# Seven block products in four more of group 0's pairs, in a one-core decoder step on Trainium2

## The chip, the cores and the metric

The kernel runs on one core of one Trainium2 chip. The metric is device time in microseconds (us). Three runs of the kernel before gave 2213.06, 2214.12 and 2216.58 us; the median is 2214.12.

## What is computed

One inference step of a two-layer decoder trunk on 576 tokens (8 samples of 8 tokens, then one prompt of 512), 1024 features, in float32. Each layer is a half-weighted SwiGLU feed-forward block (FFN), a mixer, and a second such block; layer 0's mixer is an mLSTM, layer 1's a gated linear attention (GLA). The FFN's hidden width is 2816.

```python
def rmsnorm(x, w):
    y = x * rsqrt(mean(x * x, axis=-1) + EPS)
    return y * w
def swiglu(x, w_gate, w_up, w_down):
    return (silu(x @ w_gate) * (x @ w_up)) @ w_down
for l in range(2):
    x = x + 0.5 * swiglu(rmsnorm(x, norm_w[l, 0]), ...)
    x = x + mixer[l](rmsnorm(x, norm_w[l, 1]))
    x = x + 0.5 * swiglu(rmsnorm(x, norm_w[l, 2]), ...)
out = rmsnorm(x, final_norm_w)
```

## The kernel before

**Number format.** Each float32 operand is split into a high part (fp32r, a ScalarE copy) and a low part (VectorE: value minus high part). A product of two operands is three matmuls: high x high, high x low, low x high. Weights arrive by DMA as blocks of 128 output features (512 KB, 128x1024) in `raw`, four slots; `split` on ScalarE (L1182) and VectorE (L1715) makes `w_hi` and `w_lo`.

**Layout.** Features lie on partitions. The 576 tokens are two halves of 288 columns (`FIRST`, `SECOND`), one PSUM bank each. There are 8 PSUM banks, so a pair of blocks (2 blocks x 2 halves) takes 4, and pairs alternate between banks 0 to 3 and 4 to 7.

**Phases.** An FFN is cut into three groups of 8, 8 and 6 hidden tiles of 128. Each group is a phase G (one pair per hidden tile: a gate block and an up block, evacuated to `h_hi`, `h_lo`) and a phase D (four pairs of w_down blocks, added to x). The FFNs are numbered 0 to 3; 0 and 1 stand around the mLSTM mixer, 2 and 3 around the GLA mixer. `PHASES` is the list of all phases in order; every engine walks it in its own instruction stream, and semaphores with counted values order them. Nothing but these streams and waits sets the order.

**A plain pair** (`feature_pair`, L476): per block 8 feature tiles x 3 matmuls x 2 token halves, 96 matmuls of 128x288 in all. All of phase D and all 8 pairs of group 0's G are plain. They read `xn`, the input times the norm's weights but not yet times 1/rms (`rstd`), because rstd is known only at the end of the first pair (`token_sums`, `norm_rstd`); the factor is applied on evacuation (`evac_g`, L1889 and L1891).

**A seven-product pair** (`seven_pair`, L533), groups 1 and 2 of G. The gate and up matrices, cut in even and odd feature tiles, and the activations, cut in even and odd tiles and in two token halves, are 2x2 block matrices. They are multiplied with seven block products instead of eight (a Winograd form), 7 x 4 x 3 = 84 matmuls of 128x288. That needs sums of weights (`sum_1` to `sum_4`, L1738 to L1758, VectorE, 128x512), their high and low parts (`unit_high` L1197, `unit_low` L1730), sums of activations (`t_sums`, made in phase D of group 0 with rstd already in them, in `th_hi`, `th_lo`), copies of partial results out of PSUM (`product_copy`, L1216) and four additions that join them (`part`, L1772). The last of these and the Silu (L1248, L1250) are followed by `rows_product` (L1780), the high part (L1254) and `rows_low` (L1788).

**The start.** x comes in four pieces of two tiles; ScalarE makes the high part (L1267) and the squares (L1274) of each, and behind the first piece the high parts of the first weight pair. ScalarE's first instruction waits for the norm weights and x.

## Time and profile before

| | |
|---|---|
| profiled execution, its own time | 2216.74 us |
| span | 2215.0 us, mean granted TensorE clock 0.994 |
| TensorE (PE) busy | 2176.4 us, 98%, 16504 matmuls |
| VectorE (DVE) busy | 1433.1 us, 65% |
| ScalarE (ACT) busy | 885.8 us, 40% |
| GpSimd (POOL) busy | 45.7 us, 2% |
| chain that ended last | PE 93%, DVE 4%, ACT 2%, issue 1% |
| costliest lines of the chain | L476 55%, L533 27%, L750 4% |

Times are microseconds from the span's start. An instruction's row has its start, its length, the engine, the line, and output and input with their shapes; "x2" joins two neighbours of one kind; in brackets stand the idle time of the engine before it and what ended that. Instructions of one engine overlap a little, so the spacing of starts is shorter than the lengths. A row of a stage view has the stretch, its length, then for PE, PEld (weight load), DVE, ACT and POOL the busy time and the number of instructions, then the granted TensorE clock (1.00 is 2.4 GHz), the DMA share and GB/s.

### The profile page before, as it was taken

The numbers are of one execution on the slowest core, as the hardware profiler recorded it, in microseconds if no ns is written. First come the engines' busy times: TensorE is split into PE (matmuls) and PEld (weight loads), VectorE is DVE, ScalarE is ACT, GpSimd is POOL, SyncE is SP. The second block draws the span as 40 slices with busy tenths as digits, with TensorE's granted clock in tenths as the row PEclk, the third lists the DMA queues.
The fourth block names the chain that finished last, engine by engine and source line by source line (L and its number), as shares of the span: only waits on it lengthen the run. The fifth ranks groups of instructions, "written<-read, shape, count | busy, mean of one in ns | idle before, by whom it ended". The sixth has DMA issues, their size and how long they took to land.

```text
span 2215.0 us, 40643 instructions
## 1 busy us (share of the span) xinstructions
PE 2176.4 (98%) x16504; PEld 2154.1 (97%) x16504; DVE 1433.1 (65%) x2131; ACT 885.8 (40%) x1366; POOL 45.7 (2%) x50
## 2 busy tenths in 40 slices
PE   7999999999999999999999999999999999999997
PEld 7999999999999999999999999999999899999997
DVE  5488657685555468848655884864766454788485
ACT  4235435354533334525423452544322432345252
POOL 0000000001100000000000000000011100000000
PEclk9999999999999999999999999999999999999999
DMA  5222322223332222222322222232122222223222
GB/s 185 77 81 89 114 67 86 96 88 130 108 114 77 95 77 81 90 87 88 109 80 76 86 95 95 81 100 88 47 96 87 95 77 95 76 86 104 76 86 72
DMA packets 72566, 201.42 MB, mean 91 GB/s; under 512 B 7268, under 2 KB 26980, under 8 KB 72448
## 3 DMA queue, kind: packets, MB, share of 16 engines
q1 hardware_dynamic: 72448, 199.80, 27.6%
q8 instruction: 80, 1.31, 0.2%
q14 instruction: 38, 0.31, 0.1%
HBM read 187.82 MB, written 11.95 MB: 90 GB/s over the span
## 4 chain that ended last, share of the span: by engine, by line
PE 93%; DVE 4%; ACT 2%; issue 1%; DMA 0%; POOL 0%; DVEq 0%; SPq 0%; ACTq 0%; POOLq 0%
PE ps L476 55%; PE ps L533 27%; PE ps L750 4%; PE ps L605 1%; DVE w_lo L1715 1%; PE ps L781 1%; PE ps L770 1%; PE ps L784 0%; PE ps L800 0%; ACT w_hi L1182 0%; PE ps L614 0%; PE ps L793 0%; PE ps L628 0%; PE ps L794 0%; DVE x L2514 0%
## 5 line engine op out<-in xcount | busy, mean ns | idle before, releaser
L476 PE MATMUL ps<-h_lo,w_hi 128*128 128x288 f32 x1616 | 350.9, 294 | 4.1 <-DVE h_hi L2179 4.1
L476 PE MATMUL ps<-h_hi,w_hi 128*128 128x288 f32 x1616 | 350.7, 294 | 2.5 <-DVE w_lo L1715 1.6
L476 PE MATMUL ps<-xn_hi,w_hi 128*128 128x288 f32 x1536 | 337.3, 298 | 12.4 <-DVE w_lo L1715 11.5
L476 PE MATMUL ps<-xn_hi,w_lo 128*128 128x288 f32 x1536 | 332.1, 294 | 0.0
L476 PE MATMUL ps<-xn_lo,w_hi 128*128 128x288 f32 x1536 | 331.8, 294 | 0.0
L1715 DVE TENSOR_TENSOR w_lo<-raw,w_hi 128x1024 fp32r<-128x1024 f32 x220 | 259.4, 1221 | 56.7 <-ACT w_hi L1182 54.5
L476 PE MATMUL ps<-h_hi,w_lo 128*128 128x288 f32 x1360 | 294.0, 293 | 0.0
L476 PEld LDWEIGHTS ps<-xn_hi,w_hi 128*128 128x128 f32 x1536 | 248.1, 189 | 20.5 <-issue 18.0
L476 PEld LDWEIGHTS ps<-h_lo,w_hi 128*128 128x128 f32 x1616 | 261.6, 189 | 4.8 <-DVE h_hi L2179 4.5
L476 PEld LDWEIGHTS ps<-h_hi,w_hi 128*128 128x128 f32 x1616 | 261.5, 189 | 3.5 <-DVE w_lo L1715 1.8
L533 PE MATMUL ps<-th_lo,w_hi 128*128 128x288 f32 x896 | 264.2, 295 | 0.0
L533 PE MATMUL ps<-th_hi,w_lo 128*128 128x288 f32 x896 | 263.3, 294 | 0.0
L533 PE MATMUL ps<-th_hi,w_hi 128*128 128x288 f32 x896 | 263.0, 293 | 0.0
L1182 ACT ACTIVATE w_hi<-raw 128x1024 fp32r<-128x1024 f32 x220 | 219.6, 1047 | 101.3 <-PE ps L476 76.8
L476 PEld LDWEIGHTS ps<-xn_hi,w_lo 128*128 128x128 f32 x1536 | 248.0, 188 | 0.0
L476 PEld LDWEIGHTS ps<-xn_lo,w_hi 128*128 128x128 f32 x1536 | 247.9, 188 | 0.0
L476 PEld LDWEIGHTS ps<-h_hi,w_lo 128*128 128x128 f32 x1360 | 219.1, 188 | 0.0
L1730 DVE TENSOR_TENSOR w_lo<-scratch,w_hi 128x512 fp32r<-128x512 f32 x224 | 149.6, 689 | 84.4 <-ACT w_hi L1197 84.4
L533 PE MATMUL ps<-xn_hi,w_lo 128*128 128x288 f32 x672 | 198.0, 295 | 0.0
L533 PE MATMUL ps<-xn_hi,w_hi 128*128 128x288 f32 x672 | 197.6, 294 | 0.0
L533 PE MATMUL ps<-xn_lo,w_hi 128*128 128x288 f32 x672 | 197.6, 294 | 0.0
L1931 DVE SCALAR_TENSOR_TENSOR x<-ps,x 128x1152 f32<-128x1152 f32 x52 | 70.5, 1356 | 193.0 <-PE ps L476 193.0
(276 smaller groups left out, 3731.1 us busy)
## 6 DMA issues: line engine op xcount, KB each, us to landing
raw<-in_w_gate SPq DMA_DIRECT2D x88, 512.0 KB, 3.2
raw<-in_w_up SPq DMA_DIRECT2D x88, 512.0 KB, 4.3
raw<-in_w_down SPq DMA_DIRECT2D x64, 512.0 KB, 3.6
raw<-in_w_mix SPq DMA_DIRECT2D x64, 512.0 KB, 4.3
raw<-in_w_down SPq DMA_DIRECT2D x32, 384.0 KB, 3.2
state_s<-in_state_c SPq DMA_DIRECT2D x4, 1024.0 KB, 7.1
...
```

Source lines behind the costliest of these rows:

```text
L476: ins = nc.tensor.matmul(o, a, b[:, c] if c is not None else b, start=first and j == 0, stop=last and j == 2)
L533: ins = nc.tensor.matmul(ps[:, bank, FIRST], left, b_, start=first and k == 0 and j == 0, stop=k == KT_X // 2 - 1 and j == 2, skip_group_c ...
L605: ins = nc.tensor.matmul(ps[:, bank, c * P:(c + 1) * P], left[:, ts], right[:, ts], start=True, stop=True)
L750: ins = nc.tensor.matmul(out, a[:, k, xs], b[:, 2 * half:2 * half + 2, ws], start=k == 0 and j == 0, stop=k == KT_X - 1 and j == 2)
L770: ins = nc.tensor.matmul(ps[:, 4 + c // 2, (c % 2) * DV:(c % 2 + 1) * DV], k_tok[:, c, :], v_tok[:, 1 + c, h * DV:(h + 1) * DV], start=Tru ...
L781: ins = nc.tensor.matmul(out, v_tok[:, 1 + c, vs], att(mixer, h)[:, c * P:(c + 1) * P], start=True, stop=c == 0)
L1182: nc.scalar.activation(w_hi[:, slot, :], raw[:, slot, :], ACT.Copy).then_inc(hi_done, 1)
L1715: V.tensor_tensor(w_lo[:, slot, :], raw[:, slot, :], w_hi[:, slot, :].bitcast(f32), ALU.subtract).then_inc(lo_done, 1)
L1730: return V.tensor_tensor(by_tile(unit(w_lo, half, u)), src, by_tile(unit(w_hi, half, u)).bitcast(f32), ALU.subtract)
L1931: ins = V.scalar_tensor_tensor(xs, ps[:, b:b + 4, 0:HALF_TOK], scale, xs, ALU.mult, ALU.add)
```

## The change

The last four of the eight pairs of group 0's G phase, in each of the four FFNs, are now seven-product pairs. Their sums of activations are formed from x and the norm weights without rstd, by `u_even`, `u_high` (ScalarE) and `u_sums`, `u_low` (VectorE), and lie between the work of the first four pairs. `rows_scale` applies rstd to both halves of the result. `t_sums` stays as it is, for groups 1 and 2. Two matmuls (`open_banks`) write banks 0 and 2 before the first such pair.

In every seven-product pair the order of the products is new. Three partial results are copied by ScalarE from one PSUM bank to another, where the following products add to them; one is copied to SBUF. Of the four additions one remains. The weights' four units are converted two at a time (`units_03`, `units_12`: 128x1024), gate tiles in `weights_high` and `weights_low`, and `S2`, `S3` together.

At the start ScalarE runs a small copy as soon as GpSimd's memset is done, ahead of its wait for x. The squares of piece pp follow the high parts of piece pp + 1. PE's first four pairs and the new ones are written out, the last D phase's first pair no longer runs bank by bank.

The diff without its semaphore names, access helpers and most of the removed lines (of the new functions and of VectorE's `seven_pair` the new text; TensorE's `seven_pair` comes first):

```diff
+    pe.wait_ge(lo_done, 2 * pair + 1)
     product(0, b + 1, x_tiles(even, 0), True).then_inc(product_done, 1)
-    pe.wait_ge(lo_done, 2 * pair + 1)
-    product(1, b, x_tiles(odd, 0), True).then_inc(product_done, 1)
-    pe.wait_ge(unit_lo, 5 * w + 2)
-    pe.wait_ge(copy_done, 3 * w + 1)
+    pe.wait_ge(unit_lo, 3 * w + 1)
+    product(1, b + 3, t_tiles(2), True).then_inc(product_done, 1)
+    pe.wait_ge(copy_done, 4 * w + 1)
     product(2, b + 1, t_tiles(1), False).then_inc(product_done, 1)
-    pe.wait_ge(unit_lo, 5 * w + 3)
-    product(3, b + 2, t_tiles(2), True).then_inc(product_done, 1)
-    pe.wait_ge(unit_lo, 5 * w + 4)
-    pe.wait_ge(copy_done, 3 * w + 2)
+    product(3, b, x_tiles(odd, 0), False).then_inc(product_done, 1)
+    pe.wait_ge(unit_lo, 3 * w + 2)
+    pe.wait_ge(copy_done, 4 * w + 3)
     product(0, b + 1, t_tiles(0), False).then_inc(product_done, 1)
     pe.wait_ge(lo_done, 2 * pair + 2)
-    product(1, b + 3, t_tiles(3), True).then_inc(product_done, 1)
-    pe.wait_ge(unit_lo, 5 * w + 5)
-    pe.wait_ge(copy_done, 3 * w + 3)
+    product(1, b + 2, t_tiles(3), False).then_inc(product_done, 1)
+    pe.wait_ge(unit_lo, 3 * w + 3)
+    pe.wait_ge(copy_done, 4 * w + 4)
     return product(2, b + 1, x_tiles(odd, 1), False)
...
+    def open_banks():
+        for bank in (0, 2):
+            nc.tensor.matmul(ps[:, bank, FIRST], xn_hi[:, 0, 0:P], xn_hi[:, 0, FIRST], start=True,
+                             stop=True)
...
     if consumer:
         iteration(0, first_norm=True, bank_wait=ph["base"] > 0, by_bank=(1,))
-        with pe.Fori(1, ph["pairs"] // 2) as i:
-            iteration(i)
-    elif ph["kind"] == "D" and ph["last"]:
-        iteration(0, by_bank=(0,))
         iteration(1)
+        iteration(2, seven=True, opened=False)
+        iteration(3, seven=True)
     else:
         with pe.Fori(0, ph["pairs"] // 2) as i:
-            iteration(i)
+            iteration(i, seven=ph["kind"] == "G")
...
-    w = ph["seven"] + 2 * i + half
-    act.wait_ge(sum_ready, 4 * w + 3)
-    unit_high(half, 2, by_tile(S2)).then_inc(unit_hi, 1)
-    unit_high(half, 3, by_tile(S3)).then_inc(unit_hi, 1)
...
+    act.wait_ge(sum_ready, 4 * (ph["seven"] + 2 * i + half) + 3)
+    nc.scalar.activation(units_12(w_hi, half), S32, ACT.Copy).then_inc(unit_hi, 1)
+def product_copy(dst, half, bank):
+    return nc.scalar.activation(dst, ps[:, 4 * half + bank, FIRST], ACT.Copy).then_inc(copy_done, 1)
...
-    w = ph["seven"] + 2 * i + half
-    act.wait_ge(product_done, 6 * w + 1)
-    product_copy(P1_COPY, half)
-    unit_high(half, 0, by_tile(S1)).then_inc(unit_hi, 1)
+    act.wait_ge(product_done, 6 * (ph["seven"] + 2 * i + half) + 1)
+    product_copy(ps[:, 4 * half, FIRST], half, 1)
+    if ph["group"] == 0:
+        unit_high(half, 0, by_tile(S1)).then_inc(unit_hi, 1)
 def seven_rest(j, ph, i, half, last):
     pair, w = ph["base"] + 2 * i + half, ph["seven"] + 2 * i + half
+    if ph["group"]:
+        unit_high(half, 0, by_tile(S1)).then_inc(unit_hi, 1)
     act.wait_ge(product_done, 6 * w + 2)
+    product_copy(P7_COPY, half, 3)
     act.wait_ge(raw_full[2 * half + 1], 8 * (pair - half) + 16)
     unit_high(half, 1, raw_tiles(half, 1, 1)).then_inc(hi_done, 1)
     act.wait_ge(product_done, 6 * w + 3)
-    product_copy(U2_COPY, half)
+    product_copy(ps[:, 4 * half + 2, FIRST], half, 1)
     unit_high(half, 2, by_tile(S4)).then_inc(unit_hi, 1)
     if not last:
         weights_high(ph, *step(i, half))
     act.wait_ge(product_done, 6 * w + 5)
-    product_copy(U4_COPY, half)
+    act.wait_ge(copy_done, 4 * w + 2)
+    product_copy(ps[:, 4 * half + 3, FIRST], half, 1)
     if last:
         split(PHASES[j + 1], 0, 0)
     else:
 def seven_rows(ph, i, half, last):
     m = 2 * i + half
-    w, pair, q = ph["seven"] + m, ph["base"] + m, ph["hidden"] + m
-    act.wait_ge(part_ready, 4 * w + 1)
-    nc.scalar.activation(T(0)[:, FIRST], T(0)[:, FIRST], ACT.Silu)
-    act.wait_ge(pe_done, pair + 1)
-    nc.scalar.activation(T(0)[:, SECOND], ps[:, 4 * half + 1, FIRST], ACT.Silu).then_inc(gate_done, 1)
...
+        src = ps[:, 4 * half:4 * half + 2, FIRST]
+    else:
+        act.wait_ge(gate_ready, ph["scaled"] + m + 1)
+        src = cut2(T(0))
+    nc.scalar.activation(cut2(T(0)), src, ACT.Silu).then_inc(gate_done, 1)
     if not last:
         seven_start(ph, *step(i, half))
     act.wait_ge(psum_free, pair + 1)
...
+def u_even(ph, pp):
+    act.wait_ge(ssq_done, 4 * ph["norm"] + 3)
+    if pp >= 2:
+        act.wait_ge(u_sum, 4 * ph["ffn"] + pp - 1)
+    nc.scalar.activation(T(3 + pp % 2), x[:, 2 * pp, :], ACT.Copy,
+                         scale=norm_w[:, ph["norm"], 2 * pp:2 * pp + 1]).then_inc(even_ready, 1)
+def u_high(ph, pp):
+    act.wait_ge(u_sum, 4 * ph["ffn"] + pp + 1)
+    nc.scalar.activation(th_hi[:, :, pp, :], T2(0).rearrange("p a (c n) -> p (a c) n", c=2), ACT.Copy)\
+        .then_inc(u_hi_done, 1)
...
+    else:
+        first = 2
+        split_next(j, 0, 0)
+        u_even(ph, 0)
+        u_even(ph, 1)
+        u_high(ph, 0)
+        norm_root(ph["norm"])
+        evac_g(ph, 0, 0)
+        split_next(j, 0, 1)
+        evac_g(ph, 0, 1)
+        split_next(j, 1, 0)
+        u_even(ph, 2)
+        u_high(ph, 1)
+        u_even(ph, 3)
+        u_high(ph, 2)
+        evac_g(ph, 1, 0)
+        u_high(ph, 3)
+        weights_high(ph, 2, 0)
+        sums_high(ph, 2, 0)
+        evac_g(ph, 1, 1, lambda: seven_start(ph, 2, 0))
+    with act.Fori(first, n - 1) as i:
+        seven_iteration(i)
+    seven_iteration(n - 1, last=True)
...
+act.wait_ge(zero_done, 1)
+nc.scalar.activation(rstd[SAMPLE:P, 0:1], vs_lo[SAMPLE:P, 0:1].bitcast(f32), ACT.Copy)
 act.wait_ge(norm_in, 16)
 for pp in range(4):
     act.wait_ge(x_in[pp], 16)
     xn_high(0, 2 * pp)
     xn_high(0, 2 * pp + 1)
-    squares(0, pp)
     if pp == 0:
         split(PHASES[0], 0, 0, first=True)
+    else:
+        squares(0, pp - 1)
+squares(0, 3)
 act.wait_ge(const_in, CONST_ALL)
...
+def weights_low(ph, i, half):
     m = 2 * i + half
     dve.wait_ge(hi_done, 2 * (ph["base"] + m) + 1)
+    V.tensor_tensor(units_03(w_lo, half), gate_tiles(half), units_03(w_hi, half).bitcast(f32),
+                    ALU.subtract).then_inc(lo_done, 1)
+    dve.wait_ge(unit_hi, 3 * (ph["seven"] + m) + 1)
+    V.tensor_tensor(units_12(w_lo, half), S32, units_12(w_hi, half).bitcast(f32), ALU.subtract)\
+        .then_inc(unit_lo, 1)
...
+def rows_scale(ph, i, half):
+    m = 2 * i + half
+    dve.wait_ge(pe_done, ph["base"] + m + 1)
+    V.tensor_tensor(cut2(T(0)), ps[:, 4 * half:4 * half + 2, FIRST], cut2(rstd[:, :]), ALU.mult)\
+        .then_inc(gate_ready, 1)
+    dve.wait_ge(part_ready, ph["seven"] + m + 1)
+    V.tensor_tensor(T(1), T(1), rstd[:, :], ALU.mult).then_inc(up_ready, 1)
...
+def sums_early(ph, i, half):
+    sum_3(ph, i, half)
+    sum_1(half)
+    sum_2(ph, i, half)
+    sum_4(ph, i, half)
+    weights_low(ph, i, half)
...
 def seven_pair(j, ph, i, half, before, last):
     pair, w = ph["base"] + 2 * i + half, ph["seven"] + 2 * i + half
     after = step(i, half)
+    if before and ph["group"]:
+        rows_product(ph, *before)
+    elif before:
+        rows_scale(ph, *before)
     if not last:
+        dve.wait_ge(unit_lo, 3 * w + 1)
         sum_3(ph, *after)
+    if before and ph["group"]:
+        rows_low(ph, *before)
+    elif before:
         rows_product(ph, *before)
     dve.wait_ge(sum_ready, 4 * w + 4)
+    dve.wait_ge(unit_hi, 3 * w + 2)
     unit_low(half, 0, by_tile(S1)).then_inc(unit_lo, 1)
     dve.wait_ge(hi_done, 2 * pair + 2)
     unit_low(half, 1, raw_tiles(half, 1, 1)).then_inc(lo_done, 1)
+    if before and ph["group"] == 0:
+        rows_low(ph, *before)
+    if not last:
+        dve.wait_ge(unit_lo, 3 * w + 2)
+        sum_1(after[1])
+    dve.wait_ge(unit_hi, 3 * w + 3)
     unit_low(half, 2, by_tile(S4)).then_inc(unit_lo, 1)
     if last:
+        split(PHASES[j + 1], 0, 0, (0,))
     else:
         sum_2(ph, *after)
+        dve.wait_ge(unit_lo, 3 * w + 3)
         sum_4(ph, *after)
+        weights_low(ph, *after)
+    dve.wait_ge(copy_done, 4 * w + 4)
     dve.wait_ge(product_done, 6 * w + 6)
+    V.tensor_tensor(cut2(T(1)), ps[:, 4 * half + 2:4 * half + 4, FIRST], bcast_mid(P7_COPY, 2), ALU.add)\
+        .then_inc(part_ready, 1)
+    if last:
+        split(PHASES[j + 1], 0, 0, (1,))
...
+def u_sums(ph, pp):
+    n = 4 * ph["ffn"] + pp
+    even, odd, w_odd = T(3 + pp % 2), x[:, 2 * pp + 1, :], norm_w[:, ph["norm"], 2 * pp + 1:2 * pp + 2]
+    dve.wait_ge(even_ready, n + 1)
+    if pp:
+        dve.wait_ge(u_lo_done, n)
+    own(V.tensor_tensor(T(0)[:, FIRST], even[:, SECOND], even[:, FIRST], ALU.subtract))
+    V.scalar_tensor_tensor(T(1)[:, FIRST], odd[:, SECOND], w_odd, even[:, SECOND], ALU.mult, ALU.subtract)
+    own(V.scalar_tensor_tensor(T(0)[:, SECOND], odd[:, SECOND], w_odd, T(0)[:, FIRST], ALU.mult,
+                               ALU.subtract))
+    V.scalar_tensor_tensor(T(1)[:, SECOND], odd[:, FIRST], w_odd, T(0)[:, SECOND], ALU.mult,
+                           ALU.subtract).then_inc(u_sum, 1)
+def u_low(ph, pp):
+    n = 4 * ph["ffn"] + pp
+    dve.wait_ge(u_sum, n + 1)
+    dve.wait_ge(u_hi_done, n + 1)
+    if pp == 0 and ph["ffn"] % 2:
+        dve.wait_ge(state_out, 32 * N_HEADS * (ph["ffn"] // 2 + 1))
+    V.tensor_tensor(th_lo[:, :, pp, :], T2(0).rearrange("p a (c n) -> p (a c) n", c=2),
+                    th_hi[:, :, pp, :].bitcast(f32), ALU.subtract).then_inc(u_lo_done, 1)
+    dve.wait_ge(u_lo_done, n + 1)
...
+        for i, half, sums in ((0, 0, (0,)), (0, 1, ()), (1, 0, (1, 2)), (1, 1, (3,))):
+            if (i, half) != (1, 1):
+                split_next(j, i, half)
+            for pp in sums:
+                u_sums(ph, pp)
+                u_low(ph, pp)
+            if (i, half) == (1, 1):
+                sums_early(ph, 2, 0)
+            dve.wait_ge(pe_done, ph["base"] + 2 * i + half + 1)
+            if i == half == 0:
+                norm_rstd(ph["norm"])
+            evac_g(ph, i, half)
+        seven_pair(j, ph, 2, 0, None, False)
+        seven_pair(j, ph, 2, 1, (2, 0), False)
+        first = 3
+    if first < n - 1:
+        with dve.Fori(first, n - 1) as i:
...
+    seven_pair(j, ph, n - 1, 0, (n - 2, 1), False)
+    seven_pair(j, ph, n - 1, 1, (n - 1, 0), True)
+    if ph["group"] == 0:
+        rows_scale(ph, n - 1, 1)
+    rows_product(ph, n - 1, 1)
+    rows_low(ph, n - 1, 1)
...
-    add_squares(0, pp)
     if pp == 0:
         split(PHASES[0], 0, 0)
+    elif pp > 1:
+        add_squares(0, pp - 1)
+add_squares(0, 3)
 dve.wait_ge(const_in, CONST_ALL)
 V.tensor_copy(level_mask[:, :, :].rearrange("p l n -> p (l n)"), v_tok[:, 0, :])
 dve.wait_ge(gate_hi_done, 1)
```

## Rows read from the trace of the kernel before

**Rows 1.** TensorE's waits over the whole span: who it waited for, us in total, times, longest.
```profile
PE ps L476 <- DVE w_lo L1715: 13.1, 2, 11.5
PE ps L476 <- DVE h_hi L2179: 4.1, 2, 2.1
```

**Rows 2.** The chain in order of time, FFN 1: start us, us, what.
```profile
714.48 137.55 PE ps L476 x1056
852.02 88.80 PE ps L533 x672
```

**Rows 3.** Busy time by stage, group 1 of FFN 0 (columns: see the table's text).
```profile
166.10:254.90 88.80, 88.80 (x675) 88.80 (x673) 73.09 (x126) 49.52 (x100) 0.00 (x0) 1.00 0.28 91
```

**Rows 4.** The first 30 us in order of time: start us, us, engine.
```profile
5.30 1.28 ACT L1267 ACT_TABLE_LOAD   x1 [5.30 <-DMA x<-in_x]
...
6.59 1.44 ACT L1267 ACTIVATE xn_hi<-x,norm_w 128x576 fp32r<-128x576 f32 x2
...
9.00 1.99 ACT L1182 ACTIVATE w_hi<-raw 128x1024 fp32r<-128x1024 f32 x2
...
11.47 0.82 PE L476 MATMUL ps<-xn_hi,w_hi 128*128 128x288 f32 x2 [11.47 <-DVE w_lo L1715]
...
19.47 0.53 PE L476 MATMUL ps<-xn_hi,w_hi 128*128 128x288 f32 x2 [0.87 <-DVE xn_lo L1859]
...
22.62 2.35 DVE L1715 TENSOR_TENSOR w_lo<-raw,w_hi 128x1024 fp32r<-128x1024 f32 x2
...
28.75 0.76 DVE L1874 TENSOR_SCALAR scratch<-ps 128x576 f32<-128x576 f32 x1 [3.77 <-PE ps L572]
```

**Rows 5.** Activation sums in D of group 0, FFN 0: VectorE and ScalarE.
```profile
125.47 0.46 DVE L1842 TENSOR_TENSOR scratch<-scratch 128x288 f32<-128x288 f32 x1
...
127.32 1.17 ACT L1263 ACTIVATE th_hi<-scratch 128x1152 fp32r<-128x1152 f32 x1 [0.68 <-DVE scratch L1845]
...
128.59 1.36 DVE L1854 TENSOR_TENSOR th_lo<-scratch,th_hi 128x1152 fp32r<-128x1152 f32 x1
```

**Rows 6.** VectorE in group 0, FFN 0 (first row) and FFN 1.
```profile
38.58 2.36 DVE L1715 TENSOR_TENSOR w_lo<-raw,w_hi 128x1024 fp32r<-128x1024 f32 x2 [0.20 <-ACT w_hi L1182]
...
706.74 2.35 DVE L1715 TENSOR_TENSOR w_lo<-raw,w_hi 128x1024 fp32r<-128x1024 f32 x2
...
714.51 0.76 DVE L1874 TENSOR_SCALAR scratch<-ps 128x576 f32<-128x576 f32 x1 [5.42 <-PE ps L572]
...
731.31 2.36 DVE L1715 TENSOR_TENSOR w_lo<-raw,w_hi 128x1024 fp32r<-128x1024 f32 x2 [0.19 <-ACT w_hi L1182]
...
739.74 0.76 DVE L1889 TENSOR_TENSOR scratch<-ps,rstd 128x576 f32<-128x576 f32 x1 [6.07 <-PE ps L476]
...
743.01 0.76 DVE L1898 TENSOR_TENSOR h_lo<-scratch,h_hi 128x576 f32 x1 [0.97 <-ACT h_hi L1287]
```

**Rows 7.** A seven-product pair of group 1: a copy out of a bank, two lows.
```profile
178.97 0.41 ACT L1216 ACTIVATE scratch<-ps 128x288 f32<-128x288 f32 x1 [1.17 <-PE ps L533]
...
187.45 1.29 DVE L1730 TENSOR_TENSOR w_lo<-scratch,w_hi 128x512 fp32r<-128x512 f32 x2
```

**Rows 8.** Busy time by stage behind three waits (the clock is behind the POOL column).
```profile
657.30:660.90 3.60, 3.58 (x16) 3.58 (x17) 1.54 (x4) 0.00 (x0) 0.00 (x0) 0.55 0.30 104
1760.30:1763.80 3.50, 3.45 (x15) 3.46 (x16) 1.56 (x4) 0.00 (x0) 0.00 (x0) 0.53 0.30 100
2166.00:2169.00 3.00, 3.00 (x24) 3.00 (x24) 2.61 (x3) 0.89 (x2) 0.00 (x0) 1.00 0.63 164
```

**Rows 9.** VectorE in D of group 0, FFN 0: the splits of pairs 1 and 2.
```profile
120.42 2.36 DVE L1715 TENSOR_TENSOR w_lo<-raw,w_hi 128x1024 fp32r<-128x1024 f32 x2 [0.19 <-ACT w_hi L1182]
...
138.44 2.35 DVE L1715 TENSOR_TENSOR w_lo<-raw,w_hi 128x1024 fp32r<-128x1024 f32 x2
```

**Rows 10.** The start of D of group 2, FFN 0: VectorE's parts, TensorE's stop.
```profile
372.10 1.18 DVE L1772 TENSOR_TENSOR scratch<-ps,scratch 128x288 f32<-128x288 f32 x3
...
375.78 0.54 PE L476 MATMUL ps<-h_hi,w_hi 128*128 128x288 f32 x2 [0.30 <-DVE h_lo L1788]
```

More of the change, by code:

```diff
@@ L48, in schedule @@
                 out.append(dict(kind="G", pairs=k, base=pair, ffn=ffn, norm=norm, k=KT_X, k0=k0,
-                                group=g, hidden=hidden, seven=seven, plain=hidden - seven))
-                pair, hidden, seven = pair + k, hidden + k, seven + (k if g else 0)
+                                group=g, hidden=hidden, seven=seven - (0 if g else 4), plain=4 * ffn,
+                                scaled=4 * ffn - 4))
+                pair, hidden, seven = pair + k, hidden + k, seven + (k if g else k - 4)
                 out.append(dict(kind="D", pairs=4, base=pair, ffn=ffn, norm=norm, k=k, k0=k0,
@@ L585, in iteration @@
                             pe.wait_ge(psum_free, pair - 1)
+                        if not opened and half == 0:
+                            open_banks()
                         ins = seven_pair(ph, i, half) if seven else feature_pair(ph, i, half, half in by_bank)
@@ L1279, in norm_root, with evac_g @@
                 nc.scalar.activation(rstd[:, :], T(7), ACT.Sqrt).then_inc(rstd_ready, 1)
-            def evac_g(ph, i, half):
+            def evac_g(ph, i, half, between=None):
                 m = 2 * i + half
@@ L1285, in evac_g @@
                 nc.scalar.activation(T(0), T(0), ACT.Silu).then_inc(silu_done, 1)
+                if between:
+                    between()
                 act.wait_ge(h_ready, q + 1)
@@ L1288, in evac_g @@
                     .then_inc(hh_done, 1)
+            def u_even(ph, pp):
[8 more added lines that the diff above has]
+                    .then_inc(u_hi_done, 1)
             def g_phase(j, ph):
                 n = ph["pairs"] // 2
-                def iteration(i):
-                    for half in range(2):
-                        split_next(j, i, half)
-                        if ph["group"] == 0 and half == 0 and i is 0:
-                            norm_root(ph["norm"])
-                        evac_g(ph, i, half)
                 def seven_iteration(i, last=False):
@@ L1707, in own, with split @@
                 dve.wait_ge(dve_chain, chain[0])
-            def split(ph, i, half):
+            def split(ph, i, half, blocks=range(2)):
                 pair = ph["base"] + 2 * i + half
-                for blk in range(2):
+                for blk in blocks:
                     slot = 2 * half + blk
@@ L1808, in seven_pair @@
-                dve.wait_ge(product_done, 6 * w + 2)
-                part(T(0)[:, FIRST], half, 0, P1_COPY)
-                dve.wait_ge(unit_hi, 5 * w + 5)
+                if before and ph["group"] == 0:
[4 more added lines that the diff above has]
+                dve.wait_ge(unit_hi, 3 * w + 3)
                 unit_low(half, 2, by_tile(S4)).then_inc(unit_lo, 1)
                 if last:
-                    split(PHASES[j + 1], 0, 0)
+                    split(PHASES[j + 1], 0, 0, (0,))
@@ L1814, in seven_pair @@
                 else:
-                    dve.wait_ge(unit_lo, 5 * w + 4)
-                    sum_1(ph, *after)
                     sum_2(ph, *after)
-                dve.wait_ge(copy_done, 3 * w + 2)
-                dve.wait_ge(product_done, 6 * w + 4)
-                part(T(4)[:, SECOND], half, 2, U2_COPY)
-                if not last:
-                    dve.wait_ge(unit_lo, 5 * w + 5)
+                    dve.wait_ge(unit_lo, 3 * w + 3)
                     sum_4(ph, *after)
-                dve.wait_ge(copy_done, 3 * w + 3)
@@ L1825, in seven_pair @@
-                part(T(1)[:, SECOND], half, 2, U4_COPY)
-                if not last:
-                    sums_low(ph, *after)
+                    weights_low(ph, *after)
+                dve.wait_ge(copy_done, 4 * w + 4)
                 dve.wait_ge(product_done, 6 * w + 6)
-                dve.wait_ge(part_ready, 4 * w + 2)
-                part(T(1)[:, FIRST], half, 3, T(4)[:, SECOND])
+                V.tensor_tensor(cut2(T(1)), ps[:, 4 * half + 2:4 * half + 4, FIRST], bcast_mid(P7_COPY, 2), ALU.add)\
+                    .then_inc(part_ready, 1)
@@ L1902, in g_phase @@
                 n = ph["pairs"] // 2
-                def iteration(i):
-                    for half in range(2):
-                        split_next(j, i, half)
-                        dve.wait_ge(pe_done, ph["base"] + 2 * i + half + 1)
-                        if ph["group"] == 0 and half == 0 and i is 0:
-                            norm_rstd(ph["norm"])
-                        evac_g(ph, i, half)
                 if ph["group"]:
```

89 lines of the change are left out of this document (31 added, 58 removed).

## The prediction

> **What bounds the kernel now.** I read the profile page's busy shares first: TensorE is busy for 98% of the span, so any other engine costs time only where TensorE waits for it (the shares stand in the table ahead). Next the list of TensorE's waits: behind the first 11.5 us the longest kinds are one of 1.6 us and two of 2.1, and none lies inside a group's pairs [rows 1]. Then the chain in order of time, for the price of a product in either form. In FFN 1 the last seven G pairs of group 0 and its four D pairs are 11 x 96 = 1056 products in 137.55 us, 0.1303 us each. Group 1's eight seven-product pairs are 672 in 88.80 us, 0.1321 us each [rows 2]. Last the stage view: in seven-product pairs VectorE is busy 73.09 of 88.80 us, 9.1 of 11.1 us per pair, and yet TensorE never waits [rows 3]. The kernel is bound by the number of TensorE products; what the change can lose, it loses by making VectorE late.
>
> The profiled execution took 2216.74 us (span 2215.0 and 1.7 around it), 2.6 more than the median of 2214.12. I sum gains within the profiled one and take them off the median.
>
> **Part 1, four plain pairs become seven-product pairs, in each of four FFNs.** A plain pair is 96 x 0.1303 = 12.50 us, the other 84 x 0.1321 = 11.10 us [rows 2]. 16 pairs x 1.40 = **22.4 us saved**. The two opening products per FFN are 8 x 0.13 = 1.0 us, on TensorE's own path.
>
> **Part 2, the start.** Now ScalarE waits for x until 5.30, then loads its table (1.28 us), and the first conversion begins at 6.59 [rows 4]. With a first activation that needs no input the load lies in the wait: 1.28 us earlier. The squares of the first x tiles, which fill ScalarE between 6.59 + 1.44 and 9.00, leave the way to the first weights: another 1.0. So TensorE starts at 11.47 - 2.3 = about 9.2, if the first weights have landed by 6.7. They were issued right behind the first x; if not, up to 1 us of it is lost. The later tiles of xn come earlier too; TensorE's stop before 19.47 (0.87 us) mostly goes, as VectorE hands over the last two at about 16.5, when they are wanted at 16.1. Together **3.0 us**; bounds 1.3 (table alone) and 3.3.
>
> The page of the trace has 5.30 to 6.59, so the table costs 1.28 us here. The Trainium skill (ScalarE: Activation LUTs, What ACT_TABLE_LOAD costs) counts about 1.38 us of drain beside it; by that 4.4 us would be gained at the start instead of 3.0, and the wait computed next would take back the difference.
>
> **Part 3, sums of activations in the first four pairs.** One set (u_sums, u_high, u_low) is the same shape of work as the second half of t_sums: from 125.47 to the end of 128.59 + 1.36, 4.5 us of VectorE with ScalarE's 1.17 us inside, since VectorE waits for it [rows 5]. Four sets are 18 us per FFN. VectorE has room on average, but not where they are put.
> *FFN 1 to 3.* Set 0 runs before pair 0 ends (706.74 + split 2.3 + 4.5 = 713.5, and the norm starts at 714.51): no cost. Sets 1 and 2 stand behind the split of pair 3, which starts at 731.31 [rows 6]; from there VectorE's queue is: split 2.3, two sets 9.0, evacuation of pair 2 4.0 (739.74 to 743.01 + 0.76), set 3 4.5, four weight sums 2.7 and the first half of weights_low 1.2 [rows 6, 7]. That ends at 755.0. TensorE is through pair 0 one product before 714.48 [rows 2], so through pair 3 at 714.35 + 3 x 12.5 = 751.85, opens its banks, and wants these weights at 752.1. **A new wait of 2.9 us before pair 4**, x 3 = 8.7.
> *FFN 0.* VectorE's split of pair 1 starts at 22.62, and 0.35 earlier after the change (it is behind constants and squares). Then 2.3 and set 0, 4.5: the norm starts at 29.05, against 28.75 before [rows 4], though pair 0 ends 3 us earlier. The weights of pair 2 come at 38.58 + 1.22 + 0.3 = 40.1 [rows 6], and TensorE is there at 28.4 - 3.0 + 12.5 = 37.9 (28.4: pair 0 ends some 0.3 us before the norm's first operation at 28.75): **2.2 us of waiting**, so the gain of part 2 is mostly given back. Then evacuation 45.2, split 47.5, two sets 56.5, evacuation 60.5, set 60.5 + 4.5, sums and low 68.9; TensorE is there at 40.1 + 25.0 + 0.3 = 65.4: **3.5 us**.
>
> **Part 4, the clock.** The two waits of 2.1 us in the trace, at the end of each mixer, are followed by half clock; the grant is 0.55 and 0.53 over 3.5 us, in the second of which 15 products ran instead of 27, 1.6 us lost. The wait of 1.6 us (13.1 - 11.5 of the list) was followed by granted 1.00 [rows 1, 8]. So the clock went from 2.4 to 1.2 GHz behind both stops of 2.1 us and stayed behind the one of 1.6. The five new waits are 2.2 to 3.5 us. I count a fall at four of the five: **6.4 us**; bounds 0 and 8.0.
>
> **Part 5, the seven-product pairs of group 0 in steady state.** VectorE's work per pair: four sums and three lows of 512 columns at 0.60 (1.29 for two overlapped), two lows of 1024 in 2.3, and five operations of 576 at 0.67 (two rescalings by rstd, which groups 1 and 2 don't have; product, low, part): 9.9 us, and 1.2 us of waiting for ScalarE inside [rows 7]. That is 11.1, TensorE's own pace. The tight link is the first bank copy: pair m's end, part, rescale, Silu 0.69, copy 0.41, and it must be there 3.17 us into pair m+1; laid out it ends 0.1 to 0.2 us before that. I take 0.3 us lost per FFN, 1.2 in all; bounds 0 and 0.4 in each of 12 pairs plus a later VectorE at pair 4, 9.6 in all (rivals). A copy from bank to bank is not in the trace; the nearest is a copy from bank to SBUF, 0.41 [rows 7]; at 0.2 it would save these 1.2 us, at 0.6 cost 2 more. That row's 0.41 goes into the sum. The Trainium skill (ScalarE: Activation LUTs, Step-by-step) says ScalarE writes to PSUM with less latency than to SBUF; by that the 1.2 would shrink towards 0.
>
> Groups 1 and 2: part of three operations becomes one, five lows become three with two of them wide. TensorE waits for nothing there now [rows 3] and the first copy has 0.9 us of room, so I take 0.
>
> **Part 6, the phase ends.** Into D of group 0, VectorE leaves G 5.4 us after TensorE instead of 4.0. The trace has 120.42 to 138.44 + 1.22 from its first split to pair 2's weights [rows 9], which then come 24.8 us into D and are wanted at 25.0. I take 0.1 x 4 = 0.4 lost. Into D of group 2 TensorE now waits 0.4 us for the last h_lo, behind two splits and three parts [rows 10]. One split moves behind the single part: h_lo comes 0.7 earlier, the wait goes; 0.4 x 3, and 0.6 at the last phase (wait of 1.6): 1.8 saved.
>
> **Sum:** 22.4 - 1.0 + 3.0 - 8.7 - 2.2 - 3.5 - 1.2 - 0.4 + 1.8 = 10.2, and 6.4 off for the clock: **3.8 us faster, 2210.3** (2212.9 for a profiled execution like this one).
>
> **Rivals.**
> *The clock holds.* For it: in the trace half clock follows only where TensorE idled behind small products or the mixer's tail, and 1.6 us was survived. Against: 2.1 us did it twice. Then 10.2 us are kept, with one fall 8.6: 2204 to 2205.5. This is a rival of the skill's too: by the Trainium skill (TensorE: Matmul & The Clock Gate, Why this matters for your kernels) it takes a longer idle gap than the 2.1 us that did it here, and four of the five waits would pass unharmed.
> *Slower: VectorE and ScalarE set the pace of group 0.* Mechanism: the loop part, rescale, Silu, copy, in pairs 5 to 7. It decides once each of some 20 handovers in it costs 0.05 us more than in my layout: then the copy is 0.2 to 0.4 late in each pair, and the same handovers make pair 4's wait 4 us instead of 2.9. 2.4 us x 4 = 9.6 lost: 3.8 - 9.6 = 5.8 slower, 2220. For it: 9.9 of 11.1 us busy in a queue with four cross-engine waits. Against: in groups 1 and 2, 9.1 of 11.1 run without a single wait.
> *Everything falls and the start gains nothing.* Five falls (8.0) and part 2 at 1.3, its rest in the wait anyway: about 2 us faster, 2212.
>
> **How the numbers follow.** Two results within 0.2% (4.4 us) can't be told apart. Forecast 0.45, of which 0.4 lies beyond 4.4 us faster; clock holds 0.22; slower rival 0.13, three quarters of it beyond 4.4; all falls 0.20, none beyond. Faster 0.18 + 0.22 + 0.03 for waits shorter than laid out = 0.43; slower 0.10; within 0.47. The range 2203.5 to 2217.5 takes in the clock that holds and half the way to the slower rival; the forecast's own is 2207 to 2213.
>
> **What would show it.** Right: a TensorE wait of about 2.9 us on a VectorE low (weights_low) before pair 4 of FFN 1 to 3, 3.5 in FFN 0 and 2.2 at its pair 2, half clock behind them; first product near 9.2; 11.1 us between product groups in group 0. Wrong: no wait at pair 4, waits of over 0.3 us on copies in pairs 5 to 7, granted clock 1.00 behind a wait of over 2.5 us, or waits inside groups 1 and 2.

## The result and the profile after

The changed kernel takes 2222.29 us (median of 18 runs, 2216.4 to 2225.99) against 2215.25 for the kernel before beside it: ratio 1.0035, interval 1.0028 to 1.0042. It is slower; 3.8 us faster were forecast. (One of the 18 runs of the kernel before took 5533.12 us; the median does not feel it.) The profiled execution took 2222.21 us, span 2220.4 against 2215.0. TensorE issues 184 matmuls fewer (16320) and is still busy for 98% of the span.

What TensorE waited for, in the kernel after (us in total, times, longest):

```profile
PE ps L549 <- DVE w_lo L1815: 12.8, 4, 3.5
PE ps L492 <- DVE w_lo L1770: 10.3, 2, 9.3
PE ps L492 <- DVE h_hi L2271: 4.1, 2, 2.1
PE ps L492 <- DVE xn_lo L1949: 1.0, 1, 1.0
```

The first row is new: one stop at pair 4 of each FFN, as predicted. The second has the start in it (9.3, before 11.5 [rows 1]). The third, the two waits at the mixers' ends, is as before [rows 1], and the fourth is the stop for the later tiles of xn, 0.87 us before [rows 4]. Now the chain in order of time through FFN 1 (start, duration, line, matmuls), and in its last row the exit of the second mixer; L492 is the plain pair, L549 the seven-product pair:

```profile
716.07 12.76 PE ps L492 x96
757.14 46.27 PE ps L549 x336
803.41 51.20 PE ps L492 x384
854.60 89.00 PE ps L549 x672
943.61 51.20 PE ps L492 x384
994.80 66.75 PE ps L549 x504
1765.81 54.65 PE ps L492 x408
```

and from the kernel before two rows that were not shown, the D phase of group 1 and the exit of the second mixer:

```profile
940.83 49.92 PE ps L476 x384
1760.35 56.07 PE ps L476 x408
```

Here the surprise is to be seen. The D phase of group 1 has the same 384 matmuls of the same shapes in both kernels, with no wait in either, and takes 51.20 instead of 49.92 us: 0.1333 instead of 0.1300 per matmul. The rows of groups 1's and 2's seven products are longer too (89.00 against 88.80 [rows 2]). The windows over the two D phases rule out the clock and a busier VectorE (TensorE, its weight loads, VectorE, ScalarE, GpSimd, granted clock, DMA); before, then after:

```profile
940.80:990.60 49.80, 49.80 (x386) 49.80 (x385) 19.11 (x23) 9.34 (x12) 0.00 (x0) 1.00 0.29 95
```

```profile
943.60:994.60 51.00, 51.00 (x385) 51.00 (x384) 18.51 (x19) 9.38 (x10) 0.00 (x0) 1.00 0.29 93
```

The stops, in windows of the kernel after: pair 4 of FFN 0 and what follows, and pair 2 of FFN 0 and what follows:

```profile
66.70:70.70 4.00, 0.49 (x4) 0.26 (x2) 3.92 (x6) 1.06 (x1) 0.00 (x0) 1.00 0.00 0
72.50:75.20 2.70, 2.70 (x13) 2.70 (x13) 1.79 (x3) 2.18 (x4) 0.00 (x0) 0.50 0.30 121
39.00:41.20 2.20, 0.32 (x3) 0.12 (x3) 2.01 (x3) 1.70 (x2) 0.00 (x0) 1.00 0.00 0
41.20:44.00 2.80, 2.80 (x22) 2.80 (x23) 2.64 (x4) 0.69 (x1) 0.00 (x0) 1.00 0.64 186
```

TensorE idles while VectorE is busy for 3.92 of 4.00 us. From one matmul's start to the next, less the 0.13 us that it takes anyway, the stop at pair 4 of FFN 0 costs 3.7 us (its idle part is the 3.5 of the list) and that at pair 2 costs 2.0. Half clock (1.2 GHz) follows the first and not the second.

Stage by stage, from the first matmul of each stage in the two traces, after less before, us:

| stage | change |
|---|---|
| first matmul to pair 1 of FFN 0 (28.41 to 26.21) | -2.2 |
| group 0, pairs 1 to 7: 87.77, 87.76, 87.75, 87.76 to 90.65, 87.47, 88.56, 87.46 | +3.1 |
| D phases of groups 0 and 1, eight times 49.92 to 51.19 | +10.2 |
| seven products of groups 1 and 2: 88.80 to 89.01, 66.60 to 66.75, four times | +1.4 |
| entry into D of group 2: 38.83 to 38.39 three times, 25.62 to 24.98 | -1.9 |
| three stretches of half clock in and behind the mixers that this execution had and that one not | -4.5 |
| smaller pieces | -0.7 |

The sum is the span's +5.4. The sixth line is not the change's doing: such stretches come and go between executions of one kernel (the mean granted clock of the changed kernel's 18 runs goes from 0.991 to 0.996; the row of 56.07 against 54.65 above is one such stretch). Without it the change costs 10 us, and 10.2 stand in a line where the prediction had 0.

### The profile page after: what moved, and what is told of

Its sections match the earlier page's. It is cut to its first block, busy times and chain, and to the rows that moved or that the text cites. A ratio compares the mean times of both kernels' runs of the same rounds, so it can differ in the third digit from the quotient of the medians.

```text
span 2220.4 us, 39902 instructions
## 1 busy us (share of the span) xinstructions
PE 2170.8 (98%) x16320; PEld 2148.5 (97%) x16320; DVE 1524.0 (69%) x2059; ACT 964.0 (43%) x1399; POOL 47.4 (2%) x50
## 4 chain that ended last, share of the span: by engine, by line
PE 88%; DVE 8%; ACT 3%; issue 1%; DMA 0%; POOL 0%; SPq 0%; DVEq 0%; ACTq 0%; POOLq 0%
PE ps L492 41%; PE ps L549 36%; PE ps L772 4%; PE ps L627 1%; DVE w_lo L1770 1%; DVE th_lo L1921 1%; ACT th_hi L1329 1%; PE ps L803 1%; PE ps L792 1%; PE ps L806 0%; ACT w_hi L1204 0%; PE ps L822 0%; PE ps L636 0%; DVE scratch L1966 0%; DVE scratch L1985 0%
## 5 line engine op out<-in xcount | busy, mean ns | idle before, releaser
L492 PE MATMUL ps<-h_lo,w_hi 128*128 128x288 f32 x1616 | 351.2, 297 | 4.1 <-DVE h_hi L2271 4.1
L492 PE MATMUL ps<-h_hi,w_hi 128*128 128x288 f32 x1616 | 350.7, 296 | 1.0 <-DVE w_lo L1770 1.0
L549 PE MATMUL ps<-th_lo,w_hi 128*128 128x288 f32 x1152 | 342.8, 298 | 0.0
L549 PE MATMUL ps<-th_hi,w_hi 128*128 128x288 f32 x1152 | 341.1, 296 | 0.0
L549 PE MATMUL ps<-th_hi,w_lo 128*128 128x288 f32 x1152 | 341.1, 296 | 0.0
L492 PE MATMUL ps<-h_hi,w_lo 128*128 128x288 f32 x1360 | 295.1, 296 | 0.0
L549 PE MATMUL ps<-xn_hi,w_hi 128*128 128x288 f32 x864 | 255.9, 296 | 12.8 <-DVE w_lo L1815 12.8
L492 PEld LDWEIGHTS ps<-h_lo,w_hi 128*128 128x128 f32 x1616 | 262.6, 189 | 4.8 <-DVE h_hi L2271 4.5
L492 PEld LDWEIGHTS ps<-h_hi,w_hi 128*128 128x128 f32 x1616 | 262.2, 189 | 1.2 <-DVE w_lo L1770 1.2
L549 PE MATMUL ps<-xn_hi,w_lo 128*128 128x288 f32 x864 | 255.7, 296 | 0.0
L549 PE MATMUL ps<-xn_lo,w_hi 128*128 128x288 f32 x864 | 255.5, 296 | 0.0
L492 PE MATMUL ps<-xn_hi,w_hi 128*128 128x288 f32 x1024 | 229.8, 301 | 12.2 <-DVE w_lo L1770 9.3
L492 PE MATMUL ps<-xn_hi,w_lo 128*128 128x288 f32 x1024 | 224.5, 296 | 0.0
L492 PE MATMUL ps<-xn_lo,w_hi 128*128 128x288 f32 x1024 | 224.2, 295 | 0.0
L492 PEld LDWEIGHTS ps<-h_hi,w_lo 128*128 128x128 f32 x1360 | 220.4, 189 | 0.0
L549 PEld LDWEIGHTS ps<-th_hi,w_hi 128*128 128x128 f32 x1152 | 218.8, 190 | 0.0
L549 PEld LDWEIGHTS ps<-th_hi,w_lo 128*128 128x128 f32 x1152 | 218.6, 190 | 0.0
L549 PEld LDWEIGHTS ps<-th_lo,w_hi 128*128 128x128 f32 x1152 | 218.4, 190 | 0.0
L1235 ACT ACTIVATE ps<-ps 128x288 f32<-128x288 f32 x216 | 85.3, 395 | 262.5 <-PE ps L549 261.2
```

Source lines behind the costliest of these rows:

```text
L492: ins = nc.tensor.matmul(o, a, b[:, c] if c is not None else b, start=first and j == 0, stop=last and j == 2)
L549: ins = nc.tensor.matmul(ps[:, bank, FIRST], left, b_, start=first and k == 0 and j == 0, stop=k == KT_X // 2 - 1 and j == 2, skip_group_c ...
L1235: return nc.scalar.activation(dst, ps[:, 4 * half + bank, FIRST], ACT.Copy).then_inc(copy_done, 1)
```

## The experiments

Theory at the outset: a matmul of alternating banks costs 0.1300 us when TensorE has come out of a run on a single bank without a stop since, else 0.1333. (The kernel before computes one block of pair 1 bank by bank.) Rival: where the code lies and how its loops are built.

**e1, no bank-by-bank block in the kernel before.**

```diff
-    iteration(0, first_norm=True, bank_wait=ph["base"] > 0, by_bank=(1,))
+    iteration(0, first_norm=True, bank_wait=ph["base"] > 0)
```

> The kernel before, its first pair of each group 0 no longer computing a block bank by bank (both pairs of that iteration run two banks alternately). Theory (cadence: a matmul of the plain pairs costs 0.1300 us where PE entered them out of that bank-by-bank block without a stop since, 0.1333 us otherwise): plain pairs of group 0 from pair 2 on (576 matmuls) and both D phases (768) go from 0.1300 to 0.1333, 4.5 us per FFN, the seven-product phases by 0.3 us each: +18 to +20 us, about 2234. Rival (the 0.1333 of the changed kernel comes from where its code lies or how its loops are built): D phases stay at 49.9 us, time 2215 within 1 us.

Measured: 2227.36 us, ratio 1.0053 (1.0035 to 1.0072). Its chain in FFN 1:

```profile
716.78 140.78 PE ps L476 x1056
857.56 88.81 PE ps L533 x672
946.37 49.92 PE ps L476 x384
```

The 1056 matmuls of group 0 and its D phase go from 137.55 [rows 2] to 140.78, though no loop, wait or count has changed: x 4 = 12.9 us, about the measured slowdown of 12.5. So the rival falls. But the D phase of group 1 stays at 49.92: the old seven-product pair brings TensorE into the faster spacing by itself, and my theory, which expected 18 to 20 us, had only half of it.

**e2 and its control, a stop in the kernel before.**

```diff
-    pe.wait_ge(psum_free, pair - 1)
+    pe.wait_ge(psum_free, pair if late and half == 0 else pair - 1)   # late: pair 4 only
-    with pe.Fori(1, ph["pairs"] // 2) as i:
-        iteration(i)
+    with pe.Fori(1, 2) as i:
+        iteration(i)
+    iteration(2, late=True)                                       # the control: iteration(2)
+    iteration(3)
```

> The kernel before, with TensorE made to wait at pair 4 of each group 0 for the evacuation of pair 3 (which takes a stop of about 1.5 to 2.5 us) and the loop over its last three iterations written out; nothing else. Theory (cadence lost in a stop): 4 stops of about 2 us = 8 us, and behind each the plain pairs 4 to 7 (384 matmuls) and both D phases (768) at 0.1333 instead of 0.1300 = 3.8 us per FFN, with 0.6 us of seven-product phases: +25 us, about 2240. Rival (a stop costs itself alone): +8 us, 2223, D phases at 49.9 us.

> The kernel before with the last two iterations of group 0 written out and no added stop: the control of the run with a stop at pair 4. If the stop, and not the writing out, cost the spacing there, pairs 4 to 7 and the D phase of group 0 are at 0.1300 a matmul (137.5 us for the 1056 matmuls from pair 1 on) and the time is 2215 within 2 us; if writing out costs it, 0.1333 from pair 4 on, 3.8 us per FFN, 2230.

Measured: 2231.7 us, 1.0075 (1.0057 to 1.0093); the control 2216.85 in one run. Pairs 1 to 3, then pair 4 to the end of D, then D of group 1, with the stop; and pairs 1 to the end of D in the control:

```profile
718.78 37.71 PE ps L476 x288
757.99 102.64 PE ps L476 x768
949.44 49.92 PE ps L476 x384
```

```profile
714.57 137.54 PE ps L476 x1056
```

The 768 matmuls behind the stop take 102.64 us, 0.1336 each. In the control the same 768 take 137.54 - 37.71 = 99.83, 0.1300 each. The list of waits has 6.1 us for the four stops; 2.8 x 4 = 11.2 come on top, at full clock. **A stop of 1.5 us cost 1.5 us and then 2.8 more.** The next seven-product phase puts it right again (D of group 1 is at 49.92), so the measured loss is 16.9 and not 25.

**e3, the changed kernel without its stops.** Nothing is left out; VectorE's order in group 0 becomes (several statements to a line here, the removed lines left out)

```diff
+    split_next(j, 0, 0); u_sums(ph, 0); pair_done(0); norm_variance(); u_low(ph, 0)
+    dve.wait_ge(rstd_ready, ph["norm"] + 1); evac_g(ph, 0, 0)
+    split_next(j, 0, 1); pair_done(1); evac_g(ph, 0, 1)
+    u_sums(ph, 1); split_next(j, 1, 0); u_low(ph, 1)
+    u_sums(ph, 2); sum_3(ph, 2, 0); sum_1(0); u_low(ph, 2); pair_done(2); evac_g(ph, 1, 0)
+    u_sums(ph, 3); sum_2(ph, 2, 0); sum_4(ph, 2, 0); u_low(ph, 3); weights_low(ph, 2, 0)
+    pair_done(3); evac_g(ph, 1, 1)
```

and TensorE waits for u_lo_done behind product 1 instead of ahead of it.

> The changed kernel with VectorE's order in group 0 rewoven: the first set's low part behind the reciprocal, sets 1 to 3 with a split or weight sums of pair 4 in the time in which ScalarE rounds the set, and TensorE's wait on the sets behind product 1. Nothing is left out. Both theories: the waits before pair 4 (12.8 us in 4) and before pair 2 of the first FFN (2.2) go, and the stretches at half clock behind them (about 1.4 us each). Theory (cadence): with no stop from pair 1 to the last D, plain pairs and D phases run at 0.1300, another 10.2 us in D phases and 1 to 3 elsewhere: about 2190. Rival (the spacing is set by the code, or by the two opening matmuls): D phases stay at 51.2 us, about 2202.

Measured: 2202.66 us, 0.9947 (0.9929 to 0.9964). Waits and chain:

```profile
PE ps L492 <- DVE w_lo L1770: 10.4, 2, 9.5
708.27 37.70 PE ps L492 x288
746.23 44.50 PE ps L549 x336
790.73 51.20 PE ps L492 x384
930.93 51.20 PE ps L492 x384
```

All five stops are gone and with them 19.6 us. Group 0 now takes 82.6 us for pairs 1 to 7 against 87.76 before: 5.16 us per FFN, 20.6 in all. But the D phases stay at 51.20: the stops are not what slows them in the changed kernel. The new seven-product pair, or the two opening matmuls ahead of it, is; e7 and e10 below keep the opening matmuls and reach 49.92, so it is the pair.

**e4 and e6, a bank-by-bank block at the entry of D**, in the changed kernel and in e3.

```diff
+    elif ph["kind"] == "D" and not ph["last"]:
+        iteration(0, by_bank=(0,))
+        iteration(1)
```

> The changed kernel, where the first pair of the D phases of groups 0 and 1 computes its second block bank by bank, and the two iterations are written out. Theory (the bank-by-bank block puts PE into the faster spacing): from the second pair on 0.1300 in those phases, 288 x 0.0033 = 1 us for each of 8, and 0.3 us for each seven-product phase behind: 2212 to 2214. Rival (the block does nothing by itself): 2222 within 1 us, D phases at 51.2 us.

> The reordered changed kernel, with the first pair of the D phases of groups 0 and 1 computing its second block bank by bank (both edits together, nothing left out). If the two are independent: 8 D phases of 50.2 in place of 51.2 us take 8 us off, 2202.7 to about 2194.5, ratio to before 0.991. If the faster spacing carries into the seven-product phases, 0.3 us each more, 2191. If a D phase with a bank block gets a wait of VectorE's that the block's order brings forward, 2198 or more.

Measured: e4 2214.10 us, 0.9997 (0.9987 to 1.0006); e6 2192.14, 0.9894 (0.9879 to 0.9910). D phases in e4:

```profile
803.13 50.19 PE ps L492 x384
942.32 50.19 PE ps L492 x384
```

Each D phase gives back 1.0 us, with and without the stops, and the two cures add up. In e4 the seven-product phase behind one of the four stops takes 44.73 us where the other three take 46.09 to 46.27: half clock did not follow that one.

**What differs at the entry of D.** Start-to-start times in ns of the 12 matmuls of the last product, and behind the bar of the first of D (D of group 1, FFN 0, in both kernels; the number ahead of the bar runs from the last matmul of the product to the first of D):

```
before   137 132 134 135 133 132 133 136 132 132 133 136 | 126 132 128 132 128 132 128
changed  133 133 131 134 135 133 132 133 136 132 132 133 | 133 132 132 130 132 130 132 140 131 131 131 140
```

A run on one bank has a long interval in every four. Before, the run ends behind it, and D alternates 128 and 132; in the changed kernel it ends three matmuls behind a long one, one short of the next, and every fourth interval of D is 140. Second theory: the place in this pattern at which the run ends decides. The traces already kept agree: the bank-by-bank blocks of e4 and of the kernel before end behind a long interval too (133 132 133 136, then 126 and 131 129 or 132 128 over and over), and behind the stop of e2 the pattern with 140 stands within 20 matmuls. Four runs on it:

**e5, extra matmuls beside the run**, behind the last product of group 0 and ahead of D of group 1:

```diff
+    nc.tensor.matmul(ps[:, 5, HALF_TOK:512], unit(w_hi, 1, 2)[:, 0:P], xn_hi[:, 1, 0:512 - HALF_TOK], ...)
+    nc.tensor.matmul(ps[:, 4 * half, FIRST], w_hi[:, slot, 0:P], xh[:, 0, FIRST], start=True, stop=True)
```

> The reordered changed kernel with extra matmuls whose output nothing reads, one more in each FFN (1, 2, 3, 4): behind the last product of group 0, in the same bank as that product (224 columns each), and ahead of the first D pair of group 1, in that pair's first bank (288 columns each). Theory (the matmuls fall into a pattern of four, 133 136 132 132 ns in a run on one bank, and the spacing of the alternating matmuls that follow is 0.1300 or 0.1333 by the place in that pattern at which the run ends; the kernel before leaves it behind the 136, the changed one one matmul short of that): the D phase of group 0 goes to 49.9 us in the FFN with 1 extra matmul, stays at 51.2 in that with 3 and 4. Rival (the spacing hangs on the banks' order or on the code): all D phases alike, at 51.2. The time tells nothing beyond 10 x 2 x 0.13 us added.

**e7, a longer run.** The last product repeats its last matmul 0, 1, 2, 3 times by FFN.

```diff
+    for _ in range(extra):
+        ins = nc.tensor.matmul(ps[:, bank, FIRST], left, b_, start=False, stop=True, skip_group_check=True)
```

A part of the product is so added more than once, and the results are off by it; the run is for its spacing alone.

> The reordered changed kernel, where the last product of each seven-product pair repeats its last matmul: 0 times in the first FFN, then 1, 2 and 3 times (so part of that product is added more than once). Theory (a run of matmuls on one bank goes 133 136 132 132 ns, over and over, and the alternating matmuls behind it take 0.1300 where it ends behind the 136, else 0.1333; the changed kernel's run ends three matmuls behind a 136): all 12 matmuls of the last product and one repeat end on the 136, so in the second FFN the D phases of groups 0 and 1 come to 49.9 us, in the others they stay at 51.2. Rival (the order of the banks or of the operands sets it): 51.2 in all.

**e8, other banks**, and the copies' banks to match. The two halves of the sum come out exchanged and the results are wrong; this run too is for its spacing alone.

```diff
-    product(1, b + 3, t_tiles(2), True) ... product(1, b + 2, t_tiles(3), False)
+    product(1, b + 2, t_tiles(2), True) ... product(1, b + 3, t_tiles(3), False)
```

> The reordered changed kernel with the third and fourth bank of a seven-product pair swapped in products 2 and 6 and in ScalarE's copies (the evacuation still reads them as before, so the halves of its sum come out exchanged). The banks then go 1 2 1 0 1 3 1 (before the change 1 0 1 2 1 3 1; in the changed kernel 1 3 1 0 1 2 1). Theory that the last change of banks (3 to 1, as in the kernel before) sets the spacing: D phases of groups 0 and 1 at 49.9 us, time 2202.7 - 10 = 2192. Rival (what the matmuls count, not which banks): 51.2 us, 2202.

**e9, a matmul cut in two, or one repeated elsewhere** (the cut, shortened; another one in each FFN, and in FFN 0 product 2 issues its first matmul twice).

```diff
-    nc.tensor.matmul(ps[:, bank, FIRST], left, b_, ...)
+    for c in (slice(0, 144), slice(144, HALF_TOK)):      # one matmul of the product
+        nc.tensor.matmul(ps[:, bank, c], left, b_[:, c], ...)
```

> The reordered changed kernel, with the count of TensorE's matmuls in each seven-product pair raised by one in a way that leaves the results as they are, another way in each FFN: product 2 issues its first matmul twice (its sum starts anew); the first matmul of the last product cut in two of 144 columns; the last matmul of the last product cut so; the last matmul of product 6 cut so. Theory (the place in the pattern of four at which the last run on one bank ends decides): the cuts in the last product lengthen its run to 13, as the repeat did, so the D phases of FFN 1 and FFN 2 come to 49.9 us; for a matmul more in product 2 or 6 the theory says nothing firm, since each change of bank sets the pattern anew: if only the last run's length counts they stay at 51.2. Rival (it takes 13 full matmuls of 288 columns, that is, time and not count): a cut leaves the D phases at 51.2.

D of group 0 in FFN 0, 1, 2, 3 of e7; then FFN 1 of e5 (two extra), of e8, and FFN 1 of e9 (first matmul of the run cut in two):

```profile
109.01 51.20 PE ps L492 x384
792.57 49.92 PE ps L492 x384
1184.25 51.19 PE ps L492 x384
1892.69 51.20 PE ps L492 x384
```

```profile
792.27 51.20 PE ps L492 x384
```

```profile
790.60 51.20 PE ps L492 x384
```

```profile
795.95 51.20 PE ps L492 x384
```

e7 did what the theory said: exactly one repeat brings 49.92, two and three don't, and a rule of "longer is better" can't say that. In its FFN 1 the run ends with 131 134 136, and 126 follows. e5 and e9 did not do what it said: in all their FFNs every D phase of groups 0 and 1 is at 51.2, so narrower matmuls, or full ones in the next bank or in an earlier product, don't count as members of the run. The starts of e9's FFN 1 bear that out: with its first matmul cut in two the run still ends three matmuls behind a long interval (136 133 131 134, then 132). Whether it is the full width or the time of a matmul that makes it count is not shown. e8 rules out that the last change of banks decides: it is from bank 3 to bank 1 as in the kernel before, and D stays at 51.20. (The single runs took 2202.84, 2211.83, 2200.73 and 2210.32 us in the order e5, e7, e8, e9; e7 and e9 carry a longer pair throughout, in e9 44.85 us for four pairs against 44.50 in e3.)

**e10 and e11, one full matmul more in the last run only**, in e3 and in the kernel before. It multiplies the two low parts, a term that the sum may have:

```diff
+    if fourth:    # last product of the phase's last pair
+        ins = nc.tensor.matmul(ps[:, bank, FIRST], wl, xl, start=False, stop=True, skip_group_check=True)
```

> The reordered changed kernel with one matmul more at the end of each seven-product phase (12 in all, 0.13 us each): the last product of the last pair also multiplies the low parts with each other for its last tile, a term that the sum may hold. Theory (the run on one bank must end behind the long interval): all 12 D phases start at the faster spacing, those of groups 0 and 1 take 49.9 instead of 51.2 us (8 x 1.28 = 10.2 less), that of the last group about 0.9 to 1.3 less in each FFN: 2202.7 + 1.6 - 10.2 - 4 = about 2190, ratio to before 0.9885. Rival (the repeat in all pairs was needed, not the one in the last pair): nothing but the 1.6 us, 2204.

> The kernel before with the same matmul more, at the end of the seven-product phases of groups 1 and 2. Theory: its runs end behind the long interval and now end one past it, so the D phase of group 1 goes from 49.9 to 51.2 us and the next seven-product phase with it by 0.15, that of group 2 loses about 0.2 until its stop: +6 us, 2221; the D phase of group 0 stays at 49.9. Rival (a matmul more speeds up whatever follows, or does nothing): D phases 49.9, 2216.

D phases of groups 0, 1 and 2 of FFN 1 in e10, with group 1's seven products in the second row, and D of group 1 in e11:

```profile
785.57 49.92 PE ps L492 x384
835.49 89.00 PE ps L549 x672
924.62 49.92 PE ps L492 x384
1041.42 49.91 PE ps L492 x384
```

```profile
940.93 51.19 PE ps L476 x384
```

The same matmul speeds the changed kernel's D phases up and slows those of the kernel before down, each in all four FFNs. e10 takes 2187.37 us, 0.9882 (0.9865 to 0.9899): it beats both kernels, by 26 and 35 us; from e6 it can't be told with certainty (0.9894, not in the same comparison). e11 took 2217.96 in its one run, 4.7 above the kernel before beside it; the trace has 4 x 1.27 = 5.1 in the D phases. The 0.15 us expected in the seven-product phase behind each did not come (63.43 us of its chain against 63.42). Both runs also write out the last iteration of each seven-product phase; e7 shows the effect without that.

## Why the prediction was wrong

- **Start (part 2), 3.0 expected, 2.2 measured.** The first matmul came at 9.3 instead of 9.2, and that is all of the gain; nothing of the 4.4 reckoned beside it is to be seen. The stop for the later tiles of xn, which was to go mostly, stayed: 1.0 us against 0.87.
- **Stops (part 3).** At pair 4 I had 2.9 us in FFN 1 to 3 and 3.5 in FFN 0: 3.3 and 3.7 measured from start to start (3.1 and 3.5 idle), VectorE busy through each. At pair 2 of FFN 0 I had 2.2: 2.0. Sum 14.4 against some 15.5. The place, the engine and the operation were right.
- **Clock (part 4), 6.4 expected.** Four of the five stops were followed by half clock, as counted, at 46.12 - 44.51 = 1.6 us three times and 2.7 once (47.22): 7.5. The one stop without a fall was the shortest, 2.0 us. So the rival in which the clock holds fell. By the Trainium skill (TensorE: Matmul & The Clock Gate, Why this matters for your kernels) a fall wants a longer idle gap than 2.1 us. The stop at pair 2 agrees with that, the stops of 2.1 us at the mixers' ends [rows 8] do not, and those at pair 4 came out at 3.1 us and more, too long to tell. Nothing is sharp here: one of e4's four stops at pair 4 had no fall, and the stop of 2.1 us at the second mixer's end, which had one before, had none in the kernel after (54.65 us against 56.07). My reading of the waits before was also short: I called those of 2.1 us the longest behind the start, and the same list has one of 2.2 us in the second mixer (half clock follows it too) and one of 3.7 near the end.
- **Products (part 1), 22.4 less 1.0 expected**, 20.6 measured in e3, the opening matmuls included, where nothing else is in the way.
- **Steady state of group 0 (part 5), 1.2 lost expected, 0 measured:** no wait there, and 11.13 us a pair, the same as in group 1 (89.00 / 8). So the rival in which VectorE and ScalarE set the pace of group 0 fell in its mechanism, though the result is on its side.
- **Phase ends (part 6):** no loss into D of group 0 (-0.4 expected); 1.8 expected into D of group 2, 1.9 measured.
- **The step that failed: "Groups 1 and 2: ... so I take 0"**, and with it the tacit 0 for the D phases. I looked for waits, found none, rightly, and took a matmul's price for a constant of its row. The new order of products left TensorE in the slower spacing at the end of each seven-product phase, and that cost 10.2 us in the D phases. The seven-product phases of groups 1 and 2 lost 1.4 us more, by their own new order and not by the spacing at which they are entered: in e10, with D back at 49.92, they still take 89.00. Put into the sum, with stops and clock as measured, it reads: 20.6 + 2.2 + 1.9 - 15.5 - 7.5 - 10.2 - 1.4 - 0.6 (pairs 2 and 3 of FFN 0, at the slower spacing behind their stop) = 10.5 slower. The span of that execution has 5.4, with 4.5 us of luck in the mixers' clock and 0.7 in smaller pieces; the medians have 7.0. With the D phases at 49.92 and all else as measured the change would have come out about even: e4, with D at 50.19, has the ratio 0.9997.

That the spacing, and neither a wait, the clock nor the number of matmuls, cost the 10.2 us is shown (e10 against e3, e11 against before, e7 within one kernel). What within TensorE makes the pattern of four, and why narrower matmuls don't take part, is open: the trace has only starts and modelled ends.
